# The last three weight blocks of a seven-product pair are split later, and their sums are formed later

## The chip, the cores and the metric

The kernel runs on one core of a Trainium2 chip. The metric is the device time of one execution in microseconds (us), as the median of several runs. An execution has five instruction queues that run at the same time and are each strictly in program order: TensorE (PE in the profile), VectorE (DVE), ScalarE (ACT), GpSimd (POOL) and SyncE (SP, which only issues transfers here). They meet through semaphores: an instruction adds to one when it is done, and another queue waits until it has reached a value.

## The reference

One transformer layer over 256 tokens of width 2048, in float32, and a last normalisation:

```python
h = rmsnorm(x, g_norm)
proj = einsum('bsd,de->bse', h, w_in)             # 2048 x 7704
(m_q, m_k, m_v, m_z, n_q, n_kc, n_vc, n_ks, n_vs, n_kw, n_vw, n_g, n_z) = split(proj)
o_moba = moba_attention(rope(m_q), rope(m_k), m_v)      # 8 heads of 128
y_moba = rmsnorm(o_moba * silu(m_z), g_out_moba)
o_nsa  = nsa_attention(...)                             # 8 heads, compressed, selected and window keys
y_nsa  = rmsnorm(o_nsa * silu(n_z), g_out_nsa)
out    = rmsnorm(x + concat(y_moba, y_nsa) @ w_out, g_final)
```

The part that the change is in is the four 512-wide chunks of `proj` that make m_z and n_z.

## The kernel before

**Units.** The product with `w_in` is cut into 15 chunks of 512 columns (0 to 14), and each chunk into 4 units of 512 of the 2048 inner rows. A unit (chunk, g) is a weight tile of 128 x 2048 values (1 MB). The kernel's loop counts in slots, and each engine has its own copy of this loop (`for slot in range(...)`), with what it does in a slot in a fixed order. Chunks 11 to 14 are the z chunks; after them come the units of `w_out`. Inside a queue nothing overtakes.

**Split products.** To keep float32 accuracy each product is three matmuls, high x high, low x high and high x low. ScalarE makes the high part of a unit's weights by copying it (`hi`, line 1022), and VectorE makes the low part as raw minus high (`lo`, line 1345), into one of three places of a ring. TensorE waits for the count of low parts. In this text hi(u) and lo(u) are unit number u of the stream; unit (13,1) is number 50, unit (13,2) number 51, unit (13,3) number 52.

**The seven-product pairs.** The z chunks go two by two (`PAIRS`): pair 0 is chunks 11 and 12, from slot s0 = 44 on; pair 1 is chunks 13 and 14, from s0 = 52 on. For the first 512 inner rows and both chunks, the eight block products (two halves of the tokens, two halves of these rows, two chunks) are replaced by seven products of sums, P1 to P7. They need four raw blocks of weights (128 x 1024 values each: `blk_b11`, `blk_b12`, `blk_b22`, `blk_b21`), and sums of these, that VectorE forms in place: t1 (line 1595), t2 (1599), t3 (1602) and t4 (1606). t3 writes block 4's source and needs block 3 to be split before; t4 writes block 6's source and needs block 2 to be split before. Block n is split like a unit, by `block_hi(p, n)` on ScalarE (line 1084) and `block_lo(p, n)` on VectorE (line 1591). Blocks 0 and 1 serve P1 and P5, 2 and 3 serve P6 and P3, 4 serves P7, 5 serves P2, 6 serves P4.

**TensorE around s0.** Slot s0-2: P1, P5. Slot s0-1: unit (second chunk of the previous pair, or chunk 10; last g). Slot s0 (`pair_middle`): P6, P3, then the products of unit (a,1), a being the first chunk of the pair, for the first half of the tokens (row half 0). Slot s0+1 (`pair_late`): P7, which waits for block_lo 4 and for mid_out 2; P2, which waits for block_lo 5 and for the bank's readers; the products of unit (a,1) for the second half (row half 1), which wait for mid_out 3; P4, which waits for block_lo 6. Here `mid_out` (line 1101) is a copy by ScalarE of a half-made sum out of a PSUM bank; mid_out 2 is made after P6, and mid_out 3 after P7. In pair 1, mid_out 3 also waits until GpSimd has read the buffer that it writes (`y_done` 4).

**Who else is in the queues there.** In slot 43 ScalarE evacuates chunk 10 (`evac`, line 1067), and VectorE does the row maximum of an attention job. In slot 51 comes the end of chunk 12: VectorE adds the two parts of z (`silu`, line 1561), ScalarE takes the sigmoids (line 1110), VectorE multiplies (line 1565), GpSimd multiplies the attention output `xo` with it (line 604), and in slot 52 ScalarE takes the squares of that (line 1207, `y_squares`), ahead of mid_out 3 in its queue. silu writes z only; it does not touch the blocks.

**Order of the queues before the change.** ScalarE, slot s0-1: hi, attention steps, block_hi 4, block_hi 5, then evac (pair 0) or sigmoids (pair 1); slot s0: mid_out 2, hi, squares; slot s0+1: mid_out 3, block_hi 6, hi. VectorE, pair 0: slot 43: lo(44), t3, t4, attention steps, block_lo 4, block_lo 5. Pair 1: slot 50: block_lo 2, block_lo 3, t3, t4, lo(50); slot 51: block_lo 4, block_lo 5, silu; slot 52: lo(51); slot 53: block_lo 6, lo(52). hi(50) on ScalarE is in slot 50, behind block_hi 2 and 3 and mid_out 0 and 1.

Of the kernel before, what the change touches and what calls it, by code (L numbers as in the profile page):

```python
# [56 lines left out]
PAIRS = [(11, 12, 44), (13, 14, 52)]  # L57
# [208 lines left out]
def build_layer(nc, x, positions, inv_freq, w_in, g_norm, pe_ck, pe_cv, w_ck1, w_ck2, w_cv1, w_cv2,  # L266
# [4 lines left out]
    with ExitStack() as ctx:  # L271
# [745 lines left out]
        def _(act):  # L1017
# [57 lines left out]
            def block_hi(p, n):  # L1075
                if n in (0, 3, 5):
                    act.wait_ge(blk_in[{0: 0, 3: 2, 5: 3}[n]], 16 * (p + 1))
                else:
                    act.wait_ge(blk_sum, 4 * p + {1: 1, 2: 2, 4: 3, 6: 4}[n])
                if n == 6:  # L1080
                    act.wait_ge(mid_done, 3 * p + 3)
                else:
                    act.wait_ge(unit_used, RING_NO[("early", "middle", "late")[n // 2], p] - SPL + 1)
                nc.scalar.activation(block_split(p, n)[0], block_raw(n), ACT.Copy).then_inc(blk_hi, 1)

            def mid_out_(p, i):

                if i == 1:
                    act.wait_ge(unit_used, RING_NO["early", p] + 1)
                else:  # L1090
                    act.wait_ge(mid_done, 3 * p + (1, 0, 2, 3)[i])
                if p == 0 and i == 0:
                    act.wait_ge(t_round, len(ROUNDS))
                if p and i == 0:
                    act.wait_ge(pv_done, 2 * NH)
                if p and i in (1, 2):
                    act.wait_ge(y_done, 2)
                if p and i == 3:
                    act.wait_ge(y_done, 4)
                m = (0, 1, 0, 1)[i]  # L1100
                nc.scalar.activation(mid_copy(p, i), mid_bank(p, i)[:, :], ACT.Copy, scale=rstd[:, m:m + 1]).then_inc(mid_out, 1)  # L1101
# [137 lines left out]
            for slot in range(NSLOT):  # L1239
                if slot == 0:  # L1240
                    x_hi(4)
                    x_hi(5)
                    first_hi_(2, range(UK))
                if slot == 40:
                    xs_round()
                for p in range(len(PAIRS)):
                    s0 = PAIRS[p][2]
                    if slot == s0 - 4:
                        block_hi(p, 0)
                        block_hi(p, 1)  # L1250
                    if slot == s0 - 2 and p:
                        block_hi(p, 2)
                        block_hi(p, 3)
                        mid_out_(p, 0)
                        mid_out_(p, 1)
                    if slot == s0:
                        mid_out_(p, 2)
                    if slot == s0 + 1:
                        mid_out_(p, 3)
                        block_hi(p, 6)  # L1260
                if slot and rounded_at(slot) is not None and rounded_at(slot) < NU:
                    hi(rounded_at(slot))
                if slot == PAIRS[0][2] - 2:
                    mid_out_(0, 0)
                    mid_out_(0, 1)
                    block_hi(0, 2)
                    block_hi(0, 3)
                if slot == 1:
                    x_hi(6)
                    x_hi(7)  # L1270
                if slot == 2:
                    for q in range(5):
                        act.wait_ge(x_in[q], 16)
                    for m in range(MT):
                        if m:
                            act.wait_ge(sq_done, m)
                        nc.scalar.activation(junk, xo[:, m, :], ACT.Square, accum_out=ssx[:, m:m + 1]).then_inc(sq_done, 1)
                if slot - 2 in ROUNDS and ROUNDS[slot - 2][0] == "raw":
                    q_round(slot - 2)
                if slot - 1 in CMP_TOKEN_SLOT:  # L1280
                    cmp_exp(CMP_TOKEN_SLOT.index(slot - 1))
                if slot - 1 in JOB_AT:
                    exps(JOB_AT[slot - 1])
                if slot in EARLY_AT:
                    early_hi(EARLY_AT.index(slot))
                if slot in ROUNDS:
                    round_out(slot)
                if slot == 4:
                    act.wait_ge(trig_arg, 2)
                    for i in range(2):  # L1290
                        nc.scalar.activation(trig[:, 0:MT, i * HALF:(i + 1) * HALF], trig[:, 2 + i, :].rearrange("p (m c) -> p m c", m=MT),
                                             ACT.Sin).then_inc(trig_act, 1)
                if slot - 2 in JOB_AT:
                    prob_out(JOB_AT[slot - 2])
                for p in range(len(PAIRS)):
                    if slot == PAIRS[p][2] - 1:
                        block_hi(p, 4)
                        block_hi(p, 5)
                if slot % UPC == UPC - 1 and slot < NPROJ and ACT_READS[KINDS[slot // UPC]]:
                    evac(slot // UPC)  # L1300
                if slot % UPC == UPC - 1 and slot < NPROJ and KINDS[slot // UPC] == "z":
                    sigmoids(slot // UPC)
                if slot in (CK_SLOT[3], GATE_SLOT, CK_SLOT[7]):
                    quarters_out((CK_SLOT[3], GATE_SLOT, CK_SLOT[7]).index(slot))
                if slot in CK_SUM_SLOT:
                    hidden_exp(CK_SUM_SLOT.index(slot))
                if slot in CK2_SLOT:
                    ck2_evac(CK2_SLOT.index(slot))
                if slot in CMP_SCORE_SLOT:
                    cmp_scores_out(CMP_SCORE_SLOT.index(slot))  # L1310
                if slot in CMP_T_SLOT:
                    cmp_out(CMP_T_SLOT.index(slot))
                if slot == GATE_SLOT + 1:
                    act.wait_ge(gates_sum, 1)
                    for m in range(MT):
                        nc.scalar.activation(gate[:, m, :], b_o[:, 384 + m * 32:384 + m * 32 + NGATE], ACT.Exp,
                                             scale=nrstd[:, m:m + 1]).then_inc(gate_exp, 1)
                if slot in (49, 52, 56, 60):
                    y_squares((49, 52, 56, 60).index(slot))
                for r in Y_ROUNDS.get(slot, []):  # L1320
                    y_hi(r)
                if slot in OUT_SLOT:
                    for m in range(MT):
                        final_squares(OUT_SLOT.index(slot), m)
# [8 lines left out]
        def _(dve):  # L1333
# [267 lines left out]
            def t3(p):  # L1601
                nc.vector.tensor_tensor(blk_b22, blk_b22, blk_b12, ALU.subtract).then_inc(blk_sum, 1)

            def t4(p):
                dve.wait_ge(blk_in[3], 16 * (p + 1))
                nc.vector.tensor_tensor(blk_b11, blk_b21, blk_b11, ALU.subtract).then_inc(blk_sum, 1)
# [66 lines left out]
            for slot in range(NSLOT):  # L1673
# [16 lines left out]
                for p in range(len(PAIRS)):  # L1690
                    s0 = PAIRS[p][2]
                    if slot == s0 - 4:
                        block_lo(p, 0)
                        t1(p)
                        block_lo(p, 1)
                    if slot == s0 - 2 and p:
                        block_lo(p, 2)
                        block_lo(p, 3)
                        t3(p)
                        t4(p)  # L1700
                    if slot == s0 + 1:
                        block_lo(p, 6)
                if slot > 1 and rounded_at(slot) is not None and rounded_at(slot) < NU:
                    lo(rounded_at(slot))
                if slot == PAIRS[0][2] - 2:
                    block_lo(0, 2)
                    block_lo(0, 3)
                if slot == PAIRS[0][2] - 1:
                    t3(0)
                    t4(0)  # L1710
                for p in range(len(PAIRS)):
                    if slot == PAIRS[p][2] - 3:
                        t2(p)
                if slot == 2:
                    dve.wait_ge(crows_T, 2)
                    nc.vector.tensor_copy(ccols[:, KT:], b_s[:, 0:80]).then_inc(cols_ok, 1)
                    dve.wait_ge(cols_ok, 2)
                    angles()
# [21 lines left out]
                    o_evac(JOB_AT[slot - 3])  # L1740
                if slot in JOB_AT:
                    row_max(JOB_AT[slot])
                for p in range(len(PAIRS)):
                    if slot == PAIRS[p][2] - 1:
                        block_lo(p, 4)
                        block_lo(p, 5)
                if slot % UPC == UPC - 1 and slot < NPROJ and KINDS[slot // UPC] == "z":
                    silu(slot // UPC)
                if slot in CK_SUM_SLOT:
# [44 lines left out]
```

## Time and profile before

| what | value |
|---|---|
| median of 3 runs | 502.09 us (502.05 to 502.69) |
| profiled execution, its time | 502.09 us |
| profiled execution, its span | 500.3 us |
| TensorE matmul busy | 487.5 us, 97% of the span |
| VectorE busy | 335.2 us, 67% |
| ScalarE busy | 250.2 us, 50% |
| GpSimd busy | 60.8 us, 12% |
| granted clock of TensorE, mean | 0.997 |

The span is from the first to the last instruction of the core in the profiled execution; the time of the same execution is 1.79 us longer, for what lies around it. "Busy" counts the time in which at least one instruction of the engine ran; matmuls overlap by design, so their mean durations are longer than the distance between their starts. The granted clock is given as a share of 2.4 GHz. Matmul names carry the line of the helper (647, 648, 649) and not that of the step; which step it is follows from the time and from the tiles: `ymT` holds the sums of the activations here (P5, P6, P3, P7), `xT` the activations (P1, P2, P4 and units).

### The profile page before, as it was taken

The numbers are of one execution on the slowest core, as the hardware profiler recorded it, in microseconds if no ns is written. First come the engines' busy times: TensorE is split into PE (matmuls) and PEld (weight loads), VectorE is DVE, ScalarE is ACT, GpSimd is POOL, SyncE is SP. The second block draws the span as 40 slices with busy tenths as digits, with TensorE's granted clock in tenths as the row PEclk, the third lists the DMA queues.
The fourth block names the chain that finished last, engine by engine and source line by source line (L and its number), as shares of the span: only waits on it lengthen the run. The fifth ranks groups of instructions, "written<-read, shape, count | busy, mean of one in ns | idle before, by whom it ended". The sixth has DMA issues, their size and how long they took to land.

```text
span 500.3 us, 6459 instructions
## 1 busy us (share of the span) xinstructions
PE 487.5 (97%) x2512; PEld 404.7 (81%) x2512; DVE 335.2 (67%) x535; ACT 250.2 (50%) x358; POOL 60.8 (12%) x66
## 2 busy tenths in 40 slices
PE   8999999999999999999999999999979999999993
PEld 7888778787788888888888888888758888888882
DVE  5876644345789949756687888577968766755442
ACT  5784335354556444564354384645663555445421
POOL 2340101001111202000020200002140240022020
PEclk9999999999999999999999999999999999999998
DMA  8979879685352442444344724274247677366222
GB/s 292 333 266 379 278 266 335 206 287 178 133 203 98 161 166 90 165 168 148 112 161 164 256 86 170 84 259 162 89 163 255 249 252 249 99 241 238 98 82 88
DMA packets 54543, 96.45 MB, mean 193 GB/s; under 512 B 4368, under 2 KB 13168, under 8 KB 54128
## 3 DMA queue, kind: packets, MB, share of 16 engines
q1 hardware_dynamic: 54480, 96.03, 55.2%
q8 instruction: 20, 0.33, 0.3%
q14 instruction: 11, 0.09, 0.0%
q10 hardware_dynamic: 32, 0.01, 0.0%
HBM read 93.93 MB, written 2.10 MB: 192 GB/s over the span
## 4 chain that ended last, share of the span: by engine, by line
PE 89%; DVE 4%; issue 3%; ACT 2%; POOL 1%; ACTq 0%; POOLq 0%; DVEq 0%
PE proj L647 24%; PE proj L649 23%; PE proj L648 23%; PE b_o L941 4%; PE b_t L628 2%; PE b_s L810 2%; PE b_p L910 2%; PE proj L680 2%; PE proj L686 1%; PE proj L691 1%; DVE w_lo L1591 1%; DVE w_lo L1345 1%; PE b_s L649 1%; PE b_s L647 1%; PE b_s L648 1%
## 5 line engine op out<-in xcount | busy, mean ns | idle before, releaser
L1345 DVE TENSOR_TENSOR w_lo<-w_raw,w_hi 128x2048 fp32r<-128x2048 f32 x68 | 157.3, 2314 | 93.8 <-ACT w_hi L1022 93.6
L647 PE MATMUL proj<-w_hi,xT_hi 128*128 128x512 f32 x484 | 191.1, 395 | 1.5 <-ACT rope_b L1101 0.9
L649 PE MATMUL proj<-w_hi,xT_lo 128*128 128x512 f32 x484 | 188.8, 390 | 0.0
L648 PE MATMUL proj<-w_lo,xT_hi 128*128 128x512 f32 x484 | 188.6, 390 | 0.0
L1022 ACT ACTIVATE w_hi<-w_raw 128x2048 fp32r<-128x2048 f32 x68 | 129.6, 1911 | 36.4 <-PE proj L649 24.7
L647 PEld LDWEIGHTS proj<-w_hi,xT_hi 128*128 128x128 f32 x484 | 90.9, 188 | 22.0 <-issue 2.0
L649 PEld LDWEIGHTS proj<-w_hi,xT_lo 128*128 128x128 f32 x484 | 90.9, 188 | 19.5
L648 PEld LDWEIGHTS proj<-w_lo,xT_hi 128*128 128x128 f32 x484 | 91.0, 188 | 17.8
L1161 ACT ACTIVATE pT<-b_p 128x512 f32<-128x512 f32 (+2 forms) x24 | 11.8, 490 | 53.9 <-PE b_p L910 53.9
L647 PE MATMUL proj<-w_hi,ymT_hi 128*128 128x512 f32 x80 | 31.3, 392 | 1.8 <-ACT rope_a L1101 1.8
L595 POOL TENSOR_TENSOR rope_a<-rope_a,rope_b 128x512 f32<-128x512 f32 (+1 forms) x12 | 13.1, 1111 | 159.8 <-DVE rope_b L1432 159.8
L649 PE MATMUL proj<-w_hi,ymT_lo 128*128 128x512 f32 x80 | 31.1, 389 | 0.0
L648 PE MATMUL proj<-w_lo,ymT_hi 128*128 128x512 f32 x80 | 31.1, 389 | 0.0
L1155 ACT ACTIVATE prob<-prob,nmx 128x256 f32<-128x256 f32 (+1 forms) x48 | 21.3, 447 | 7.7 <-DVE nmx L1528 7.7
L1524 DVE CUSTOM_DVE_ANT_0 prob<-b_s,mask 128x256 f32<-128x256 f32 (+1 forms) x48 | 15.2, 353 | 8.1 <-PE b_s L649 8.1
L647 PEld LDWEIGHTS proj<-w_hi,ymT_hi 128*128 128x128 f32 x80 | 15.0, 188 | 5.2 <-ACT rope_a L1101 2.2
L649 PEld LDWEIGHTS proj<-w_hi,ymT_lo 128*128 128x128 f32 x80 | 15.0, 188 | 3.1
L648 PEld LDWEIGHTS proj<-w_lo,ymT_hi 128*128 128x128 f32 x80 | 15.0, 188 | 3.0
L604 POOL TENSOR_TENSOR xo<-xo,rope_a 128x512 f32<-128x512 f32 x4 | 7.5, 1902 | 79.8 <-DVE xo L1548 64.0
L1137 ACT ACTIVATE Q<-b_t 128x512 f32<-128x512 f32 x9 | 5.4, 597 | 20.2 <-PE b_t L628 20.2
L617 POOL TENSOR_TENSOR Q<-Q,KV 128x512 f32<-128x512 f32 x6 | 7.7, 1299 | 58.8 <-ACT rope_c L1222 58.8
L582 POOL TENSOR_TENSOR rope_a<-rope_a,rope_b 128x512 f32<-128x512 f32 x4 | 6.2, 1551 | 67.4 <-DVE rope_b L1445 67.4
(249 smaller groups left out, 554.3 us busy)
## 6 DMA issues: line engine op xcount, KB each, us to landing
w_raw<-in_w_in_dram SPq DMA_DIRECT2D x53, 1024.0 KB, 4.9
w_raw<-in_w_out_dram SPq DMA_DIRECT2D x16, 1024.0 KB, 5.0
xo<-in_w_ck_dram SPq DMA_DIRECT2D x4, 1024.0 KB, 8.0
xo<-in_w_cv_dram SPq DMA_DIRECT2D x4, 1024.0 KB, 8.0
w_raw<-in_w_in_dram SPq DMA_DIRECT2D x12, 256.0 KB, 6.5
Q<-in_x_dram SPq DMA_DIRECT2D x1, 2048.0 KB, 9.6
out_dram<-Q SPq DMA_DIRECT2D x8, 256.0 KB, 2.9
xo<-in_x_dram SPq DMA_DIRECT2D x3, 512.0 KB, 7.7
```

The source lines that it names most:

```text
L595: nc.gpsimd.tensor_tensor(rope_a[:, m, 0:w], rope_a[:, m, 0:w], rope_b[:, m, 0:w], ALU.add).then_inc(rope_sum, 1)
L628: last = nc.tensor.transpose(bank_[:, n * P:(n + 1) * P], src, ident[:, :])
L647: nc.tensor.matmul(dst, a_hi, b_hi, start=first, stop=False, skip_group_check=goes_on)
L648: nc.tensor.matmul(dst, a_hi, b_lo, start=False, stop=False, skip_group_check=goes_on)
L649: return nc.tensor.matmul(dst, a_lo, b_hi, start=False, stop=last, skip_group_check=goes_on)
L680: return nc.tensor.matmul(dst, x_hi, w_hi_, start=u == 0 and k == 0, stop=False)
L941: last = nc.tensor.matmul(b_o[:, m * P:(m + 1) * P], a, v, start=n == 0, stop=n == len(prods) - 1)
L1022: nc.scalar.activation(split_of(u)[0], w_raw[:, u % RAW], ACT.Copy).then_inc(hi_ready, 1)
L1155: last = nc.scalar.activation(prob[:, b, c0:c1], prob[:, b, c0:c1], ACT.Exp, bias=nmx[:, b, n:n + 1], scale=SCALE, accum_out=sums[:, b, n: ...
L1161: nc.scalar.activation(pT[:, j % 2, 0:width(j)], b_p[:, 0:width(j)], ACT.Copy).then_inc(pt_out, 1)
L1345: nc.vector.tensor_tensor(wl, w_raw[:, u % RAW], wh.bitcast(F32), ALU.subtract).then_inc(lo_ready, 1)
L1524: nc.vector.tensor_tensor_reduce(out=prob[:, j % 2, c0:c1], in0=b_s[:, c0:c1], in1=mask[:, slice(*mask_cols(j, n))], scale=1.0, scalar=NEG ...
```

## The change

Two groups of steps move; none is added or taken away. In both pairs `block_hi` 4 and 5 go from the end of slot s0-1 to slot s0 on ScalarE, the first ahead of mid_out 2 and the second behind it. `block_lo` 4 and 5 go from slot s0-1 to the head of slot s0 on VectorE. In pair 1, t3 and t4 go from slot 50, where they stand ahead of lo(50), to slot 51, behind it and ahead of silu; in pair 0 they stay where they are. So the order becomes, on ScalarE: slot s0-1: evac or sigmoids; slot s0: block_hi 4, mid_out 2, block_hi 5, hi, squares. On VectorE in pair 1: slot 50: block_lo 2, block_lo 3, lo(50); slot 51: t3, t4, silu; slot 52: block_lo 4, block_lo 5, lo(51). All waits stay as they are inside the steps.

```diff
@@ ScalarE's loop
                     if slot == s0:
+                        block_hi(p, 4)
                         mid_out_(p, 2)
+                        block_hi(p, 5)
...
                 if slot - 2 in JOB_AT:
                     prob_out(JOB_AT[slot - 2])
-                for p in range(len(PAIRS)):
-                    if slot == PAIRS[p][2] - 1:
-                        block_hi(p, 4)
-                        block_hi(p, 5)
@@ VectorE's loop
                     if slot == s0 - 2 and p:
                         block_lo(p, 2)
                         block_lo(p, 3)
-                        t3(p)
-                        t4(p)
+                    if slot == s0:
+                        block_lo(p, 4)
+                        block_lo(p, 5)
                     if slot == s0 + 1:
                         block_lo(p, 6)
...
-                if slot == PAIRS[0][2] - 1:
-                    t3(0)
-                    t4(0)
                 for p in range(len(PAIRS)):
                     if slot == PAIRS[p][2] - 3:
                         t2(p)
+                    if slot == PAIRS[p][2] - 1:
+                        t3(p)
+                        t4(p)
...
                 if slot in JOB_AT:
                     row_max(JOB_AT[slot])
-                for p in range(len(PAIRS)):
-                    if slot == PAIRS[p][2] - 1:
-                        block_lo(p, 4)
-                        block_lo(p, 5)
```

## Rows read from the trace of the kernel before

**Rows 1.** Waits of TensorE, whole span: us in total, times, longest

```profile
PE proj L647 <- ACT rope_a L1101: 1.8, 1, 1.8
PE proj L647 <- ACT rope_b L1101: 0.9, 1, 0.9
PE proj L647 <- DVE w_lo L1345: 0.6, 1, 0.6
```

**Rows 2.** Timeline of TensorE: start, duration, step, in brackets the idle time before

```profile
361.21 0.50 PE L647 MATMUL proj<-w_hi,xT_hi 128*128 128x512 f32 x1 [0.58 <-DVE w_lo L1345]
...
363.84 0.39 PE L649 MATMUL proj<-w_hi,xT_lo 128*128 128x512 f32 x1
366.05 0.50 PE L647 MATMUL proj<-w_hi,ymT_hi 128*128 128x512 f32 x1 [1.81 <-ACT rope_a L1101]
...
367.54 0.39 PE L647 MATMUL proj<-w_hi,xT_hi 128*128 128x512 f32 x1
...
369.98 0.50 PE L647 MATMUL proj<-w_hi,xT_hi 128*128 128x512 f32 x1 [0.92 <-ACT rope_b L1101]
```

**Rows 3.** Timeline of VectorE around the second pair

```profile
347.70 3.27 DVE L1345 TENSOR_TENSOR w_lo<-w_raw,w_hi 128x2048 fp32r<-128x2048 f32 x1 [0.24 <-ACT w_hi L1022]
350.90 2.30 DVE L1599 TENSOR_TENSOR blk_b<-raw_e,blk_b 128x1024 f32<-128x1024 f32 x1
...
357.74 1.22 DVE L1606 TENSOR_TENSOR blk_b<-wv,blk_b 128x1024 f32<-128x1024 f32 x1
358.88 2.28 DVE L1345 TENSOR_TENSOR w_lo<-w_raw,w_hi 128x2048 fp32r<-128x2048 f32 x1
361.08 1.22 DVE L1591 TENSOR_TENSOR w_lo<-raw_e,w_hi 128x1024 fp32r<-128x1024 f32 x1
...
363.35 1.40 DVE L1561 SCALAR_TENSOR_TENSOR rope_b<-proj,rstd,rope_b 128x512 f32<-128x512 f32 x2
364.87 1.29 DVE L1565 TENSOR_TENSOR rope_b<-rope_b,prob 128x512 f32<-128x512 f32 x2
367.83 2.91 DVE L1345 TENSOR_TENSOR w_lo<-w_raw,w_hi 128x2048 fp32r<-128x2048 f32 x1 [1.67 <-ACT w_hi L1022]
```

**Rows 4.** Timeline of ScalarE around the second pair

```profile
356.29 1.91 ACT L1022 ACTIVATE w_hi<-w_raw 128x2048 fp32r<-128x2048 f32 x1
358.10 1.05 ACT L1084 ACTIVATE w_hi<-raw_e 128x1024 fp32r<-128x1024 f32 x1
...
364.21 1.21 ACT L1110 ACTIVATE prob<-rope_b 128x512 f32<-128x512 f32 x2 [4.11 <-DVE rope_b L1561]
365.32 0.67 ACT L1101 ACTIVATE rope_a<-proj,rstd 128x512 f32<-128x512 f32 x1
365.89 1.91 ACT L1022 ACTIVATE w_hi<-w_raw 128x2048 fp32r<-128x2048 f32 x1
...
368.63 0.63 ACT L1207 ACTIVATE rope_c<-xo 128x512 bf16<-128x512 f32 x1 [0.23 <-POOL xo L604]
...
369.26 0.67 ACT L1101 ACTIVATE rope_b<-proj,rstd 128x512 f32<-128x512 f32 x1
```

**Rows 5.** Timeline of GpSimd in two short stretches, one product a row

```profile
348.79 3.33 POOL L604 TENSOR_TENSOR xo<-xo,rope_a 128x512 f32<-128x512 f32 x1
...
365.64 1.70 POOL L604 TENSOR_TENSOR xo<-xo,rope_b 128x512 f32<-128x512 f32 x1 [13.52 <-DVE rope_b L1565]
```

**Rows 6.** Timelines of ScalarE and of TensorE in the first pair

```profile
309.93 1.06 ACT L1084 ACTIVATE w_hi<-raw_e 128x1024 fp32r<-128x1024 f32 x1 [3.63 <-PE proj L649]
...
311.84 1.25 ACT L1067 ACTIVATE KV<-proj,rstd 128x512 f32<-128x512 f32 x2
...
316.61 0.40 PE L647 MATMUL proj<-w_hi,ymT_hi 128*128 128x512 f32 x1
```

**Rows 7.** Stretches at the end: PE, PEld, DVE, ACT, POOL busy, PEclk, DMA

```profile
492.00:493.00 1.00, 0.31 (x2) 0.00 (x0) 0.65 (x1) 0.00 (x0) 0.00 (x0) 1.00 0.00 0
...
497.00:498.00 1.00, 0.00 (x0) 0.00 (x0) 0.00 (x0) 0.00 (x0) 0.00 (x0) 0.77 1.05 371
```

## The prediction

> **What bounds the kernel now.** I read the list of what TensorE waited for first. Behind the start it names three waits, 3.3 us together, and all three are in the second pair of chunks (13 and 14) [rows 1]. So TensorE sets the end nearly everywhere, and outside this pair a step on another engine is worth nothing as long as it stays in time. The TensorE timeline places the waits [rows 2]. The first is in front of the row-half-0 products of unit (13,1), which start at 361.21 and wait for the residual (low part) that VectorE makes of that unit; I call it lo(50). The second is in front of product P7 at 366.05, which waits for the copy mid_out 2. The third is in front of the row-half-1 products at 369.98, which wait for mid_out 3. Inside a run of products the starts are 0.24 us apart (361.21 to 363.84 is eleven steps), and six products with a restart take 1.49 us (366.05 to 367.54). A late or early start at 369.98 goes to the end unchanged, because no wait follows it.
>
> Then I read the queues that feed these three points: VectorE [rows 3], ScalarE [rows 4], GpSimd [rows 5]. They are strictly in program order. Now VectorE does t4 (357.74), lo(50) (358.88), block_lo 4 (361.08), block_lo 5, and the two parts of silu (363.35 and 364.87). ScalarE does hi(50) (356.29 to 358.20), block_hi 4 (358.10), block_hi 5, then it waits for silu and does sigmoids (364.21), mid_out 2 (365.32), hi(51) (365.89), two squares (the second at 368.63), mid_out 3 (369.26). The reader is to see that block_hi 4 and 5 and block_lo 4 and 5 lie in time that is otherwise a wait: ScalarE stood 4.11 us in front of the sigmoids even so.
>
> **The first pair.** Here the sum of the work in front of hi(45) is the same, only its order changes: the two mv evacuations (1.25 us, at 311.84) go ahead of block_hi 4 (309.93) [rows 6]. Two block copies take 1.91 us from start to start (309.93 to 311.84), so 0.95 each. block_hi 4 starts at about 311.1, block_hi 5 behind mid_out at about 312.6, and it ends at 313.7. With 1.22 us for a block residual, block_lo 4 ends near 313.4 and block_lo 5 near 314.9. P7 is at 316.61 and waits for nothing [rows 6]; 1.7 us or more are left. I take 0; the cover is what TensorE computes between the end of unit (10,3), on which the 309.93 copy started, and P7, 6.7 us later. If it were gone the cost would be at most the 1.1 us by which block_hi 4 is later, and there is no gain to be had since TensorE doesn't wait here.
>
> **The second pair, step by step.** Nothing before 356.6 moves.
> - t3 and t4 go behind lo(50). In VectorE's queue lo(50) is then next at 356.6 (where t3 starts now, 1.14 before t4), but it needs hi(50), which ends at 358.20. hi(50) is where it was. lo(51) started 0.03 us behind its copy (365.89 + 1.91 = 367.80, start 367.83), so lo(50) starts at 358.23 instead of 358.88, 0.65 earlier, and VectorE stands still for 1.6 us that t3 and t4 filled. The row-half-0 products start at about 360.56 and end 0.65 us earlier. That is the gain of this edit, and only if it's kept.
> - t3, t4 follow: lo takes 2.20 from start to start (358.88 to 361.08), t3 and t4 1.14 each (357.74 to 358.88), so silu starts at 358.23 + 2.20 + 2.28 = 362.71, against 363.35. Moving block_lo 4 and 5 behind silu takes 2.27 from this way, and the two moved sums and the idle time put 1.63 back: 0.64 is left.
> - ScalarE: sigmoids end their turn at 365.32 - 0.64 = 364.68. Now block_hi 4 is there: 364.68 to 365.73. mid_out 2: 365.63 to 366.30 (now 365.99). block_hi 5: 366.20 to 367.25 (mid_out takes 0.57 from start to start, 365.32 to 365.89). hi(51): 367.16 to 369.07. So two block copies, 1.91 us, that lay in the wait are now on ScalarE's way to mid_out 3.
> - mid_out 3: 369.26 - 0.64 + 1.91, less the up to 0.23 us that the second square waited for GpSimd, gives 370.3; TensorE started 0.72 behind the start of this copy, so at 371.0, against 369.98.
> - block_lo 4 could start at 365.76, and here it meets GpSimd. Its two products for chunk 12 (xo times z) follow silu, and the first ends at 365.64 + 1.70 - 0.64 = 366.70. What happens then the rows at 347.70 show: lo, otherwise 2.29, took 3.27, since it was issued while the first GpSimd product ran; the second GpSimd product was issued at 348.79 and took 3.33, to 352.12, that is to 1.15 behind VectorE's end at 350.97; t2, otherwise 1.22 like t4, was issued at 350.90 and ended at 353.20, 1.08 behind GpSimd. They took turns and nothing overlapped [rows 3, 5]. The same turns here: block_lo 4 ends at 366.70 + 1.22 - 0.15 = 367.77, the second GpSimd product at 368.92, block_lo 5 at 370.00. (The 0.15 is by how much 350.97 lies ahead of 348.79 + 2.29, with the 0.04 that a start lies ahead of the end before it.)
>
> The Trainium skill, "SBUF — State Buffer", "Who interferes with whom", calls this an exclusive lock between GpSimd and a VectorE instruction that has two inputs in SBUF, where the loser blocks for the whole instruction. The trace agrees: 3.27 us against 2.29 [rows 3]. By this rule the way over block_lo decides; without it the way over mid_out 3 would.
>
> - TensorE: P7 needs block_lo 4 (new: so far mid_out 2 was last). A product started 0.05 behind the end of its residual (358.88 + 2.28 = 361.16, start 361.21). P7 starts at 367.82, P2, which needs block_lo 5, at 370.05, and row half 1 at 370.05 + 1.49 = 371.54, 0.5 behind mid_out 3's own time. Against 369.98 this is +1.56 us. Behind it, lo(51) ends at 372.2 and block_lo 6 at about 373.3; P4 needs it only at 371.54 + 12 products, about 374.4. hi(52) waits for TensorE and moves with it. SP's loads are freed by residuals: that for unit (13,1) comes 0.65 earlier, that for (13,2) 1.5 later, as its reader does.
>
> Bounds of what no row shows: the turns with GpSimd cost between 0 (block_lo 4 and 5 alone: then mid_out 3 decides, +1.0) and one product of GpSimd more (if its second product goes first, block_lo 4 ends at about 369.0 and block_lo 5 at 370.1, +1.7). I take +1.56, since the only row with the same three instructions in line has this order. **Sum:** 0 (pair one) - 0.65 (row half 0) + 2.21 (what is lost again behind it) = +1.56. The profiled execution has 502.09 us with a span of 500.3; that is the median of the runs, and so 502.09 + 1.56 = 503.65, forecast 503.6, own range 503.3 to 504.0.
>
> **Rivals.**
> - mid_out 3 alone decides, with no clash on the shared access: +1.0, 503.1. For it: block_lo is short, and the order could fall well. Against: VectorE is issued in the middle of GpSimd's first product.
> - The clock falls in the longer stop. TensorE would stand still from about 363.6 to 367.8, 4.2 us; now its longest stop is 1.81. At the end of the span its last product is over at 492.31 and the granted clock goes from 1 to 0.5 inside 497 to 498 (0.77 there), so some 5.2 us later [rows 7]. 4.2 is under this, but near. If it fell to 1.2 GHz, P7 would take 2.8 instead of 1.49 and hold P2 until 370.7, and P2 another 1.3: row half 1 at 373.5, +3.5, 505.6, and more if it stayed low longer. The Trainium skill, "TensorE: Matmul & The Clock Gate", "HAM oscillation — how this bites in real kernels", warns of just such stops in front of short runs of products; no stop inside this kernel shows it.
> - Not slower: lo(50) gets in at once. If hi(50) were ready when VectorE comes to it, the whole way over t3, t4, silu and the sigmoids would be up to 1.6 us earlier than I have it, and row half 1 would start at 371.54 - 1.6 = 369.9: 502.0, no change, and 501.5 if the clash with GpSimd went well too. It decides as soon as hi(50) ends before 356.7 instead of 358.2; each part of this counts one for one. For it: hi(50) stands behind a t2 that took 2.30 instead of 1.22 because of GpSimd [rows 3], and so another turn order there would move it. Against: the change touches nothing before that.
>
> **Chances.** Forecast 0.53, mid_out 3 alone 0.20, clock 0.12, not slower 0.15. A measurement of this kernel tells 0.2%, 1.0 us, from no change, so the bound is at 503.1. Slower: all of the forecast, the clock and about half of the second case, 0.76. Same: the rest of that case and the larger part of the last, 0.18. Faster: 0.06. The range 501.9 to 504.7 leaves out the clock and the best of the last case. The likeliest is 503.6.
>
> **What would show it.** Right: no product in pair one waits; lo(50) starts near 358.2 with VectorE idle before it; row half 0 starts near 360.6; silu near 362.7; P7 names block_lo (VectorE) as what it waited for, near 367.8; P2 has a second wait, near 370; row half 1 near 371.5; block_lo 4 or 5 is longer than 1.22. Wrong: P7 before 366.1, a granted clock below 1 near 368, or a difference that comes in after 372.

## The result, and the profile after

The changed kernel takes 505.18 us (median of 4 runs, 504.56 to 505.44), the kernel before beside it 502.31; the ratio is 1.0054, 95% interval 1.0037 to 1.0073. So it is slower by 2.87 us, where 1.56 was forecast; the time lies above the range. The profiled execution has 504.46 us, the least of the five that were timed, and a span of 502.7, 2.4 more than before; so its trace shows less of the loss than a typical execution has.

What TensorE waited for, whole span (us in total, times, longest), which answers to [rows 1]:

```profile
PE proj L647 <- DVE w_lo L1589: 4.3, 1, 4.3
PE proj L965 <- POOL ident L551: 1.5, 1, 1.5
```

Three waits have become one, for the low part of block 4 (line 1589 is line 1591 of before). The timeline of TensorE, with the places of [rows 2]:

```profile
363.35 0.39 PE L649 MATMUL proj<-w_hi,xT_lo 128*128 128x512 f32 x1
368.00 0.47 PE L647 MATMUL proj<-w_hi,ymT_hi 128*128 128x512 f32 x1 [4.27 <-DVE w_lo L1589]
368.31 0.51 PE L648 MATMUL proj<-w_lo,ymT_hi 128*128 128x512 f32 x1
368.62 0.63 PE L649 MATMUL proj<-w_hi,ymT_lo 128*128 128x512 f32 x1
369.04 0.63 PE L647 MATMUL proj<-w_hi,ymT_hi 128*128 128x512 f32 x1
...
370.32 0.68 PE L647 MATMUL proj<-w_hi,xT_hi 128*128 128x512 f32 x1
...
372.45 0.39 PE L647 MATMUL proj<-w_hi,xT_hi 128*128 128x512 f32 x1
```

P7 starts at 368.00, and from the third product on the starts are 0.43 us apart instead of 0.23. P2 starts at 370.32 with no wait, although block_lo 5 was done only at 370.09: P7 itself took until then. Row half 1 starts at 372.45 (369.98 before). The stretches show why; the columns are length, busy time of PE, PEld, DVE, ACT and POOL, the granted clock, DMA share, GB/s:

```profile
367.00:368.00 1.00, 0.00 (x0) 0.03 (x1) 1.00 (x2) 1.00 (x2) 1.00 (x1) 1.00 0.00 0
368.00:369.00 1.00, 1.00 (x3) 0.80 (x4) 1.00 (x1) 1.00 (x1) 1.00 (x1) 0.72 0.00 0
369.00:370.00 1.00, 1.00 (x4) 0.66 (x2) 1.00 (x1) 0.91 (x4) 0.01 (x1) 0.50 0.00 0
370.00:371.00 1.00, 1.00 (x4) 0.70 (x3) 1.00 (x2) 1.00 (x3) 0.32 (x1) 0.50 0.00 0
371.00:372.00 1.00, 1.00 (x4) 0.76 (x4) 1.00 (x1) 1.00 (x2) 1.00 (x1) 0.58 0.06 16
372.00:373.00 1.00, 1.00 (x6) 0.83 (x5) 1.00 (x2) 0.20 (x1) 0.91 (x2) 1.00 0.00 0
```

The granted clock is 0.50 (1.2 GHz) from 368.4 to 371.8, right where the products start again after a stop of 4.27 us. In the kernel before it stayed at 1.00 in the same place:

```profile
366.00:367.00 1.00, 0.95 (x4) 0.82 (x5) 0.16 (x1) 1.00 (x1) 1.00 (x1) 1.00 0.00 0
```

VectorE, against [rows 3]:

```profile
358.35 2.29 DVE L1343 TENSOR_TENSOR w_lo<-w_raw,w_hi 128x2048 fp32r<-128x2048 f32 x1 [1.55 <-ACT w_hi L1022]
360.56 1.22 DVE L1600 TENSOR_TENSOR raw_e<-raw_e,nv 128x1024 f32<-128x1024 f32 x1
361.69 1.22 DVE L1604 TENSOR_TENSOR blk_b<-wv,blk_b 128x1024 f32<-128x1024 f32 x1
362.83 1.41 DVE L1559 SCALAR_TENSOR_TENSOR rope_b<-proj,rstd,rope_b 128x512 f32<-128x512 f32 x2
364.35 1.29 DVE L1563 TENSOR_TENSOR rope_b<-rope_b,prob 128x512 f32<-128x512 f32 x2
365.88 1.98 DVE L1589 TENSOR_TENSOR w_lo<-raw_e,w_hi 128x1024 fp32r<-128x1024 f32 x1 [0.23 <-ACT w_hi L1084]
367.78 2.31 DVE L1589 TENSOR_TENSOR w_lo<-wv,w_hi 128x1024 fp32r<-128x1024 f32 x1
```

lo(50) waits 1.55 us for its copy; block_lo 4 and 5 take 1.98 and 2.31 instead of 1.22. ScalarE, against [rows 4], and the second product of GpSimd, against [rows 5]:

```profile
363.69 1.21 ACT L1110 ACTIVATE prob<-rope_b 128x512 f32<-128x512 f32 x2 [5.37 <-DVE rope_b L1559]
...
367.27 1.91 ACT L1022 ACTIVATE w_hi<-w_raw 128x2048 fp32r<-128x2048 f32 x1
...
370.56 0.69 ACT L1101 ACTIVATE rope_b<-proj,rstd 128x512 f32<-128x512 f32 x1
```

```profile
366.73 2.28 POOL L604 TENSOR_TENSOR xo<-xo,rope_b 128x512 f32<-128x512 f32 x1
```

This execution is 0.11 us later than that of before from its start on (355.58 against 355.47 for block_lo 3). With that taken off, nearly every forecast start is within 0.1 us: lo(50) 358.24 (forecast 358.23), silu 362.72 (362.71), block_lo 4's start 365.77 (365.76), P7 367.89 (367.82), mid_out 3 370.45 (370.3). The pair's other end isn't: row half 1 at 372.34 instead of 371.54. In the first pair P7 waits for nothing, as forecast.

### The profile page after: what moved, and what is told of

It reads as the page before. It is cut to its first block, busy times and chain, and to the rows that moved or that the text cites. A ratio compares the mean times of both kernels' runs of the same rounds, so it can differ in the third digit from the quotient of the medians.

```text
span 502.7 us, 6459 instructions
## 1 busy us (share of the span) xinstructions
PE 488.8 (97%) x2512; PEld 405.9 (81%) x2512; DVE 336.9 (67%) x535; ACT 250.3 (50%) x358; POOL 62.0 (12%) x66
## 4 chain that ended last, share of the span: by engine, by line
PE 89%; issue 3%; DVE 3%; ACT 2%; DMA 1%; ACTq 0%; POOLq 0%; POOL 0%; DVEq 0%
PE proj L647 24%; PE proj L649 24%; PE proj L648 24%; PE b_o L941 4%; PE b_t L628 2%; PE b_s L810 2%; PE b_p L910 1%; PE proj L680 1%; PE proj L686 1%; PE proj L691 1%; DMA xo<-in_x_dram 1%; PE b_s L649 1%; PE b_s L647 1%; PE b_s L648 1%; ACT w_hi L1022 1%
```

## The experiments

All were timed beside the kernel before, in three groups, and each difference below is against the median of its own group: 502.55 for fill14, fill6, blocks_moved and sums_moved, 502.52 for fill14_smallpool, early_copies, early_all and early_all_t4, 502.63 for before_fill6, sums_fill14 and the two `_sq` kernels. Starts out of different traces are compared after the shift between them is taken off, read from block_lo 3, which lies ahead of all the changes.

**fill14.** The changed kernel with idle products in the stop:

```diff
                 a, b, _ = PAIRS[p]
+                if p:
+                    pe.wait_ge(pt_out, len(JOBS))
+                    for _ in range(14):
+                        nc.tensor.matmul(b_p[:, :], xT_hi[:, 0, 0:P], xT_hi[:, 0:2, :].rearrange("p k t -> p (k t)"),
+                                         start=True, stop=True)
                 pe.wait_ge(mid_out, 4 * p + 3)
```

> The changed kernel with 14 idle products (128x512, into the free bank b_p, result unused) in TensorE's queue between row half 0 and P7 of the second pair; nothing else moves. In the changed kernel TensorE stood 4.27 us there and the granted clock was 0.50 from 368.4 to 371.8. Theory (queues and clock): 14 products at 0.227 us fill about 3.2 us, so no stop is longer than about 1.2 us, the clock stays at 1.00, P7 still starts near 368.0 (it waits for block_lo 4), P2 has a wait of its own near 370.2, row half 1 near 371.7 instead of 372.45. Time: kernel before + 1.6, about 503.9. Rival (the clock is a sideshow and the loss is all in the queues): time as the changed kernel, 505.2, with row half 1 near 372.4.

Measured: 504.08 us, ratio 1.0029 (1.0017 to 1.0040), so +1.53. TensorE's timeline:

```profile
364.01 3.33 PE L752 MATMUL b_p<-xT_hi 128*128 128x512 f32 x14
368.51 0.47 PE L647 MATMUL proj<-w_hi,ymT_hi 128*128 128x512 f32 x1 [1.17 <-DVE w_lo L1594]
...
370.76 0.47 PE L647 MATMUL proj<-w_hi,xT_hi 128*128 128x512 f32 x1 [0.62 <-DVE w_lo L1594]
...
372.21 0.39 PE L647 MATMUL proj<-w_hi,xT_hi 128*128 128x512 f32 x1
```

This trace is 0.58 us later than that of before (block_lo 3 at 356.05). With that off, P7 is at 367.93 and comes when it did in the changed kernel (367.89), row half 1 is at 371.63 (forecast 371.54), and the forecast second wait in front of P2 is there; the clock stays at 1.00. 14 products that compute nothing win back 1.3 us (2.87 - 1.53): that is the clock's part, and 1.53 is the queues' (forecast 1.56).

**fill6.** The same with `range(6)`.

> The same with 6 idle products, about 1.4 us, so a stop of about 2.9 us is left in front of P7. Theory: the length of the stop decides; 2.9 lies between 1.81 (no fall, kernel before) and 4.27 (fall), I expect no fall and 503.9. Rival 1: the clock falls as soon as a stop is clearly longer than 1.81, then 505 and a clock of 0.50 near 368. Rival 2 (not the clock): 505.2 without a fall.

Measured: 505.31 us (503.99 to 505.77), ratio 1.0049 (1.0037 to 1.0062). The stop in front of P7 was 2.93 us, and the clock fell in it:

```profile
366.00:367.00 1.00, 0.00 (x0) 0.00 (x0) 1.00 (x1) 1.00 (x2) 1.00 (x2) 1.00 0.00 0
367.00:368.00 1.00, 0.17 (x1) 0.20 (x2) 1.00 (x2) 1.00 (x2) 1.00 (x1) 0.64 0.00 0
```

The expectation fails and rival 1 holds: the clock falls in a stop of 2.9 us. What the fall costs is another matter, and this trace, of the fastest of the five executions (503.99), shows it:

```profile
367.83 0.76 PE L647 MATMUL proj<-w_hi,ymT_hi 128*128 128x512 f32 x1 [2.93 <-DVE w_lo L1594]
...
370.53 0.47 PE L647 MATMUL proj<-w_hi,xT_hi 128*128 128x512 f32 x1
```

P7 took 2.70 us instead of 1.49, but block_lo 5, which P2 needs, was done only at 369.91 anyway, and the clock was back soon after P2 had started (its products are 0.23 us apart from the second on). Row half 1 (371.99 here, 372.04 with the shift of 0.05) is only 0.41 later than in fill14. The other four executions took longer (504.51 to 505.77) and left no trace.

**blocks_moved.** Only block_hi and block_lo 4 and 5 move:

```diff
                     if slot == s0 - 2 and p:
                         block_lo(p, 2)
                         block_lo(p, 3)
+                        t3(p)
+                        t4(p)
```

(against the changed kernel, with t3 and t4 in slot s0-1 for pair 0 alone).

> Only block_hi and block_lo 4 and 5 move, as in the change; t3 and t4 of the second pair stay in front of lo(50). Theory: silu comes 2.27 us earlier (near 361.2), row half 0 at 361.3 as before, P7 waits for block_lo 4 near 366.3, P2 near 368.5, row half 1 near 370.0: no change, 502.3 (within 0.4), clock 1.00. Rival: the two block copies on ScalarE's way to mid_out 3 cost their 1.9 us by themselves, then 504.2.

Measured: 502.53 us (502.0 to 503.2), ratio 1.0003 (0.9994 to 1.0012): no change. In the profiled execution (502.35) P7 waited 2.0 us for block_lo 4, P2 0.61 for block_lo 5, and the clock stayed at 1.00 until the end of the work. But the median hides two kinds of execution: six of the eleven have 502.00 to 502.53, with a mean clock of 0.994 or 0.995, and five have 502.8 to 503.2, with 0.992 (more on this in the last section). The block copies use time that silu's earlier start gives.

**sums_moved.** Only t3 and t4 of the second pair move behind lo(50); the blocks stay as before.

> Only t3 and t4 of the second pair move behind lo(50); block_hi and block_lo 4 and 5 stay in front of silu and of the sigmoids. Theory: block_hi 4 waits for t3 (361.7), block_lo 5 ends near 365.1, silu starts near 365.0 (363.35 before), mid_out 2 ends near 367.7 and lets P7 go there, mid_out 3 near 370.9, row half 1 near 371.6. TensorE stands about 4.1 us in front of P7. If the clock falls as in the changed kernel: about 505; if not: 503.9. So the moved sums are the part that costs. Rival: the sums are harmless (their gain of 0.65 in front of row half 0 stays): 501.6 to 502.3.

Measured: 505.46 us (504.20 to 505.67), ratio 1.0051 (1.0038 to 1.0063). The wait has another name, and the same size:

```profile
PE proj L647 <- ACT rope_a L1101: 4.1, 1, 4.1
```

```profile
373.21 0.60 PE L647 MATMUL proj<-w_hi,xT_hi 128*128 128x512 f32 x1
```

```profile
366.00:367.00 1.00, 0.00 (x0) 0.00 (x0) 0.88 (x2) 0.92 (x2) 0.00 (x0) 0.92 0.00 0
367.00:373.00 6.00, 5.08 (x12) 4.02 (x13) 4.18 (x4) 5.52 (x9) 4.48 (x4) 0.50 0.01 3
```

The clock is low through all of P7 and P2, and row half 1 starts at 373.21 (373.05 with the shift of 0.16). This part of the change alone makes the whole loss.

**sums_fill14.** sums_moved with fill14's 14 products.

> Only t3 and t4 moved (sums_moved), with the 14 idle products in front of P7. Theory: the clock stays up, P7 near 367.9, row half 1 near 371.6, 1.6 us more than before, 504.1: the moved sums alone make all that the change loses in the queues, and the clock the other 1.3. Rival: 505.4 as sums_moved.

Measured: 503.92 us, ratio 1.0029 (1.0018 to 1.0039), so +1.29, where 1.6 was expected; P7 had a wait of 0.99, row half 1 of 0.89, the clock no fall there. The clock's part is 1.6 us here (2.91 - 1.29, each against its own group).

**fill14_smallpool.** fill14 with `cw = 16 if n == 1 else CW` as the width of GpSimd's two products for chunk 12, so that they hardly meet VectorE. The kernel leaves out the other 496 columns of these products, so only its times are of use.

> fill14 (the changed kernel with 14 idle products in front of P7) with GpSimd's two products for chunk 12 cut from 512 to 16 columns; it leaves out the rest of these products. It tells what the turns between GpSimd and VectorE cost when the clock stays up. Theory: block_lo 4 and 5 take 1.22 us each instead of 2.03 and 2.32, P7 starts at 367.7 (368.51 in fill14), P2 has no wait left or under 0.2, and mid_out 3 decides: row half 1 starts near 371.6 instead of 372.2, so 0.5 us less than fill14, 503.5. Rival (the turns aren't the cause of the long block_lo): block_lo stays near 2, time as fill14, 504.1.

Measured: 503.38 us, ratio 1.0019 (1.0011 to 1.0028), +0.86. VectorE's two blocks, and TensorE's wait:

```profile
365.95 1.23 DVE L1595 TENSOR_TENSOR w_lo<-raw_e,w_hi 128x1024 fp32r<-128x1024 f32 x1 [0.23 <-ACT w_hi L1090]
367.47 1.23 DVE L1595 TENSOR_TENSOR w_lo<-wv,w_hi 128x1024 fp32r<-128x1024 f32 x1 [0.29 <-ACT w_hi L1090]
```

```profile
371.29 0.50 PE L648 MATMUL proj<-w_hi,xT_hi 128*128 128x512 f32 x1 [0.82 <-ACT rope_b L1107]
```

The turns with GpSimd were what stretched the blocks, and they cost 0.7 us (1.53 - 0.86). Without them mid_out 3 decides, as the first rival said (+1.0).

**before_fill6.** The kernel before with 6 idle products in its stop of 1.81 us.

> The kernel before with 6 idle products in front of P7 of the second pair. They end inside its stop of 1.81 us. It tells whether such products change anything where no long stop is. Theory: no change, 502.5, clock the same. Rival (the products help by themselves, so that fill14's gain says nothing on the clock; or the stop of 1.81 already costs clock in some executions): below 502.2.

Measured: 502.31 us, ratio 0.9996 (0.9987 to 1.0005): no change of the time that can be told. So idle products don't speed the kernel up by themselves, and fill14's gain does speak of the clock. The mean clocks do differ: all eleven executions have 0.994 to 0.997, while nine of the seventeen of the kernel before beside them have 0.992 or 0.993. That is for the rival's second half, that the stop of 1.81 us already costs clock in some executions; the last section comes back to it.

**early_copies.** Against the kernel before (block_lo 6 on VectorE moves with block_hi 6):

```diff
-            return (mid_c1[p], rope_a[:, 1, :], rope_a[:, 0, :], rope_b[:, 1, :])[i]
+            return (mid_c1[p], rope_a[:, 1, :], rope_a[:, 0, :], raw_e[:, 1, :] if p else rope_b[:, 1, :])[i]
...
-                if p and i == 3:
-                    act.wait_ge(y_done, 4)
...
-                    if slot == s0:
+                    if slot == s0 and p == 0:
                         mid_out_(p, 2)
-                    if slot == s0 + 1:
+                    if slot == s0 + (1 - p):
                         mid_out_(p, 3)
                         block_hi(p, 6)
...
                         block_hi(p, 5)
+                        if p:
+                            mid_out_(p, 2)
```

> The kernel before with ScalarE's and VectorE's order of the second pair changed otherwise: mid_out 2 goes ahead of the sigmoids of chunk 12 (ScalarE waits there for 4.1 us), mid_out 3 is written to a buffer that GpSimd doesn't read (raw_e), so without the wait for y_done 4, and it goes with block_hi 6 ahead of hi(51) and the squares; block_lo 6 goes ahead of lo(51). Theory: P7 follows row half 0 at once (364.1), row half 1 starts near 366.9 instead of 370.0, P4 at 369.6 without a wait, but lo(51) ends only near 371.9, so about 0.9 is lost in front of unit (13,2): 2.2 less than before, 500.3. Rival: other waits take all of it (bank of chunk 12, or lo(51) later still): 502 or more.

Measured: 500.35 us, ratio 0.9957 (0.9944 to 0.9969), 2.2 less than before, as expected; 0.54 us was left in front of unit (13,2).

**early_all** adds hi(51) behind mid_out 2 in slot 51, and `if i == 12: lo(51)` between silu's parts. **early_all_t4** takes t4 there too, and block_lo 6.

> early_copies, and hi(51) also ahead of the sigmoids, lo(51) between the two parts of silu. Theory: only the 0.7 us in front of row half 0 are left of the waits, GpSimd's and the squares' work falls later but has 6 us: 3.1 less than before, 499.4. Rival: lo(51) in that place delays GpSimd's product, and through the scale of y the transposes of slot 54: nothing gained against early_copies.

> early_all with t4 taken from in front of lo(50) and put between the two parts of silu, t3 left where it is, and block_lo 6 ahead of silu's second part. Theory: t3 fits into the time in which VectorE waits for hi(50), so lo(50) starts at 358.2 and row half 0 no longer waits; nothing else gets late: 3.7 less than before, 498.8. Rival: block_hi 6, which needs t4, comes too late for P4 and costs what was gained: 499.4 or more.

Measured: 500.25 us (ratio 0.9956, 0.9944 to 0.9968) and 501.48 us (0.9982, 0.9972 to 0.9991). The second median stands for no execution: six of the twelve have 500.71 to 500.84, with a mean clock of 0.994 to 0.997, and six have 502.13 to 502.6, with 0.991 or 0.992. Both kernels miss what I expected, 499.4 and 498.8, and early_all's rival names the reason: in early_all TensorE waited 0.81 us at 377.4 for the scaled y, in early_all_t4 1.97 us at 378.0 (profiled at 500.82). ScalarE's squares wait for GpSimd's product, which silu's late second part holds up, and hi(52) stood behind the squares.

**early_all_sq, early_all_t4_sq**: the same two with `hi(52)` ahead of the squares.

> early_all with hi(52) ahead of the squares of chunk 12 on ScalarE. In early_all hi(52) stood behind squares that waited for GpSimd until 372.4, so lo(52) and behind it the scaling of y on VectorE came late, and TensorE waited 0.81 us for it at 377.4. Theory: hi(52) starts near 369.4, lo(52) near 371.3, y is scaled as soon as GpSimd has the factor (near 374), the transposes of slot 54 wait for nothing: 3.0 us less than the kernel before, 499.5. Rival: the factor itself comes too late: 500.2 as early_all.

> early_all_t4 with the same hi(52) ahead of the squares. Theory: no wait in front of row half 0, and the transposes of slot 54 wait at most 0.2 us for the scaled y: 3.5 us less than before, 499.0. Rival: GpSimd's products (until 372.4 there) and the factor behind them still come 1 us or more too late for the transposes: 500.3 or more.

Measured: 499.11 us (ratio 0.9934, 0.9921 to 0.9946) and 499.18 us (the same ratio). early_all_sq is the fastest here, 3.5 us under the kernel before, and beats both kernels; what is left of TensorE's waits in it:

```profile
PE proj L965 <- POOL ident L551: 1.5, 1, 1.5
PE proj L647 <- DVE w_lo L1348: 0.6, 1, 0.6
```

The t4 variant takes away the 0.6 and gets 0.49 in front of the transposes of slot 54 instead, so nothing is gained.

## Why the prediction was wrong, point by point

- **First pair, 0.** Right: block_hi 5 ended at 313.72 (forecast 313.7) and no product waited.
- **lo(50) 0.65 earlier.** Right, and given back at once, as said. Moving t3 and t4 out of time that VectorE spends waiting for hi(50) is what makes silu, the copies and P7 late; sums_moved shows that it is enough by itself.
- **ScalarE's way to mid_out 3, +1.03.** Right: mid_out 3 started at 370.45 in the changed kernel, and where it alone decides the time is up by 0.86 (fill14_smallpool).
- **Turns with GpSimd.** Right in order and size: block_lo 4 and 5 took 1.98 and 2.31 us, where the steps have 2.0 (365.76 to 367.77) and 2.3 (from 367.7 to 370.00); they are 0.7 us of the time.
- **The sum, +1.56.** It is the cost of the queues, 1.53 in fill14. The step that failed is TensorE's own speed behind the stop: the sum takes 1.49 us for six products, so P7 and P2 at 2.4 GHz, and leaves the fall of the clock to a rival. P7 took 2.32 us (368.00 to 370.32) and P2 2.13 (370.32 to 372.45). I gave this rival 0.12 because the clock had fallen 5.2 us after the last product [rows 7] and "4.2 is under this, but near". It fell in the profiled execution, and the time of all four runs lies above every run of fill14 (504.56 or more against 504.25 or less), with a mean clock of 0.989 to 0.992 against 0.994 to 0.997. What that row showed was one delay, not a limit; a limit can't be had from one fall.
- **The price of that rival, +3.5.** Its working, row half 1 held by a P7 and a P2 at half speed, was right in kind and too high: +2.36 in the profiled execution and +2.87 by the medians. In the trace the fall came after P7's second product had started (368.4) and the clock was back before P2 was through (371.8), where I had both at the lower level throughout. Where both were, in sums_moved, row half 1 is 3.07 later than before (373.05 against 369.98). So the price goes by how far the fall reaches: against a trace with the stop filled, row half 1 is 0.41 later in fill6, where P7 alone is slow and fills P2's wait, 0.71 in the changed kernel, where part of P2 is slow too (372.34 against 371.63), and 1.34 in sums_moved (373.05 against 371.71). The 504.7 at the upper end left this case out.
- **A stop of 1.81 us as the harmless case.** The working compares 4.2 us with a stop that showed no fall in one trace. The mean clocks on record speak against that: in a good part of its executions the kernel before seems to have a fall too (last section).

The Trainium skill, "TensorE: Matmul & The Clock Gate", "Why this matters for your kernels", warns of gaps between bursts of matmuls as what drops the throughput inside a kernel. The runs agree: stops of 2.93 us (fill6), 4.13 (sums_moved) and 4.27 each have a fall in their trace. I had cited another section of the same page with the same warning, and weighed one row of my own above it.

What stays open: there is one trace of each kernel, so why fill6 takes 503.99 us in one execution and 505.77 in another is argued from the traces of others and not shown. Part of the 0.3 us by which sums_fill14 came out under its expectation is in what it is compared with: against the eight executions of before in its group that have a mean clock of 0.994 or more (median 502.46) it is +1.5. The rest is open; its own wait rows agree with the steps.

## What to carry to other kernels

A step in an in-order queue that fills a wait is free where it is and full price anywhere else; before moving it, ask what the engine does with the time it leaves. When a change lengthens a stop of TensorE, sum the stop first, because the clock may fall in it, and idle products in the stop are a cheap test of that. Ask then what the slow products would hold up: a fall that only fills the next wait costs little. And look at the single executions and not only at their median: two groups of times with two mean clocks hint at a fall that comes in some of them. The largest gain lay in neither order compared but in the copies that waited behind work that they didn't need.

## What the runs showed of the hardware that I had not expected

After the last product the clock fell at very different delays: 5.2 us in the kernel before (492.31 to 497.5), but 2.1 us in blocks_moved (492.59 to 494.7, from a mean of 0.85 in this stretch):

```profile
494.00:495.00 1.00, 0.00 (x0) 0.00 (x0) 0.33 (x3) 0.22 (x1) 0.55 (x1) 0.85 0.00 0
```

In early_all_sq it was 2.3 us, and the 14 traces have 2.0 to 5.2. In the changed kernel the fall even came 0.4 us after the products had started again.

The mean clock of an execution shows whether there was a fall inside it, though one has to know what the end takes. In the 14 traces the clock was low at the end for 2.8 to 6.0 us, which alone gives a mean of 0.994 to 0.997, and the eleven traces without a fall inside have just these means. The three with one have 0.990 to 0.992. All timed executions, by TensorE's longest stop in the trace (behind the start of the kernel):

| kernel | longest stop | executions at 0.993 or less | their times | times of the others |
|---|---|---|---|---|
| before, in the three groups | 1.81 us | 23 of 56 | 502.55 to 502.79, median 502.67 | median 502.39 |
| early_all_t4 | 1.97 | 6 of 12 | 502.13 to 502.60 | 500.71 to 500.84 |
| blocks_moved | 2.01 | 5 of 11 | 502.80 to 503.20 | 502.00 to 502.53 |
| fill6 | 2.93 | 5 of 5 | 503.99 to 505.77 | |
| sums_moved | 4.13 | 5 of 5 | 504.20 to 505.67 | |
| the changed kernel | 4.27 | 5 of 5 | 504.46 to 505.44 | |
| the eight others | 1.17 or less | 0 of 55 | | |

So a stop of 1.8 to 2.0 us seems to have a fall in about half of the executions, and the same kernel then comes in two groups of times: 0.3 us apart for the kernel before, 1.5 for early_all_t4. No trace shows such a fall, as the profiled executions of these three kernels were all of the other group; that it lies in the stop is inferred from the eight kernels that have no such stop, above all from before_fill6, which differs from before in the idle products alone. It also means that the gains and losses above, taken against the median of before, lean on a mixed figure: against its executions at 0.994 or more, fill14 is +1.66 (504.08 - 502.42) instead of +1.53.

When VectorE and GpSimd both have work for the shared access, they take turns one instruction at a time: 1.98 and 2.31 us on one side, 2.28 on the other.
